# Placing the routing weights of a PEER layer: two fp32r products with the one-hots where one fp32 product stood

## What is computed

```
cand = (v1[..., :, None] + v2[..., None, :]).reshape(TOKEN_CHUNK, PEER_HEADS, PEER_TOPK * PEER_TOPK)
top_s, top_c = lax.top_k(cand, PEER_TOPK)
e1 = jnp.take_along_axis(i1, top_c // PEER_TOPK, axis=-1)
e2 = jnp.take_along_axis(i2, top_c % PEER_TOPK, axis=-1)
expert = e1 * PEER_KEYS + e2
g = jax.nn.softmax(top_s, axis=-1)
u = jnp.take(expert_u, expert, axis=0)
act = jax.nn.gelu(jnp.einsum('thkd,td->thk', u, xc).astype(jnp.float32), approximate=False)
w = (g * act).astype(xc.dtype)
return jnp.einsum('thk,thkd->td', w, jnp.take(expert_v, expert, axis=0))
```

## Time and profile before

| what | us |
|---|---|
| median of 3 runs (lowest, highest) | 2684.39 (2683.01, 2688.0) |
| the profiled execution: its own time | 2680.22 |
| its span, first to last instruction | 2678.4 |
| PE busy in the span | 2513.1 (94%) |
| PE weight loads / DVE / ACT / POOL busy | 2326.6 / 1722.5 / 1218.6 / 1241.4 |
| chain that ended last: share of PE / DVE / POOL | 73% / 8% / 8% |
| placing stretches, layer 0 and layer 1 | 997.4 to 1251.8 and 2053.0 to 2307.3 |

### The profile page before, as it was taken

One profiled execution on the slowest core, in us unless ns is written; L12 is line 12 of the kernel. 1 busy time (PEld: TensorE's weight loads), 2 busy tenths in 40 slices (PEclk: granted clock), 3 DMA queues, 4 the chain that ended last, 5 costly groups with the idle time before them and its releaser, 6 DMA issues.

```text
span 2678.4 us, 45632 instructions
## 1 busy us (share of the span) xinstructions
PE 2513.1 (94%) x17562; PEld 2326.6 (87%) x17562; DVE 1722.5 (64%) x3009; ACT 1218.6 (45%) x2090; POOL 1241.4 (46%) x506
## 2 busy tenths in 40 slices
PE   7998899868789999999999999998999999999998
PEld 6998799858689999999888888888999999988887
DVE  5558487468934976666766774662795666555555
ACT  5334333334434544444444444554544444445444
POOL 4437588625357996665000002446798666300000
PEclk8899899978889999999999998999999999999999
DMA  4325477754245554444877773334555444555664
GB/s 162 95 74 163 133 246 242 259 184 142 63 124 173 181 192 144 149 150 157 268 258 252 251 266 113 104 102 142 179 176 173 150 145 148 167 194 190 192 193 142
DMA packets 125335, 457.84 MB, mean 171 GB/s; under 512 B 13904, under 2 KB 14288, under 8 KB 124752
## 3 DMA queue, kind: packets, MB, share of 16 engines
q1 hardware_dynamic: 124848, 450.73, 52.1%
q10 hardware_dynamic: 288, 4.33, 0.4%
HBM read 453.95 MB, written 1.05 MB: 170 GB/s over the span
## 4 chain that ended last, share of the span: by engine, by line
PE 73%; DVE 8%; POOL 8%; issue 6%; DMA 3%; ACT 2%; POOLq 0%; SPq 0%; DVEq 0%; ACTq 0%
PE ms L1190 26%; PE mm L1152 17%; PE mm L751 16%; POOL low L1683 8%; PE ms L1172 4%; PE mm L758 2%; PE mm L769 1%; DVE work L1716 1%; DMA ring<-w_ffn_up 1%; PE mm L781 1%; DVE work L1722 1%; DMA ring<-w_ffn_down 1%; ACT high L1363 1%; DVE work L2013 1%; DVE parts L1716 1%
## 5 line engine op out<-in xcount | busy, mean ns | idle before, releaser
L1683 POOL TENSOR_TENSOR low<-ring,high 128x1024 fp32r<-128x1024 f32 (+1 forms) x502 | 1241.2, 2486 | 1069.8 <-ACT high L1363 891.7
L1565 ACT ACTIVATE high<-ring 128x1024 fp32r<-128x1024 f32 x506 | 535.9, 1059 | 356.8 <-PE ms L1190 321.7
L1152 PE MATMUL mm<-hs,high 128*128 128x256 f32 x4096 | 524.2, 281 | 3.4 <-ACT high L1363 3.4
L1190 PE MATMUL ms<-high,wts 128*128 128x512 f32 x2048 | 511.1, 392 | 0.0
L1152 PEld LDWEIGHTS mm<-hs,high 128*128 128x128 f32 x4096 | 490.2, 188 | 3.8 <-issue 3.8
L2179 DVE TENSOR_TENSOR low<-ring,high 128x1024 fp32r<-128x1024 f32 x256 | 313.4, 1225 | 248.7 <-ACT high L1565 248.4
L1190 PEld LDWEIGHTS ms<-high,wts 128*128 128x128 f32 x2048 | 384.2, 188 | 83.2
L1363 ACT ACTIVATE high<-ring 128x1024 fp32r<-128x1024 f32 (+1 forms) x252 | 259.1, 1032 | 254.2 <-PE mm L751 109.8
L751 PE MATMUL mm<-hs,high 128*128 128x256 f32 x2608 | 344.8, 287 | 16.5 <-ACT high L1363 16.3
L751 PEld LDWEIGHTS mm<-hs,high 128*128 128x128 f32 x2608 | 324.4, 195 | 21.3 <-ACT high L1363 17.9
L1152 PE MATMUL mm<-hs,low 128*128 128x256 f32 x2048 | 278.5, 278 | 10.1 <-POOL low L1683 9.9
(11 more groups left out here) (285 smaller groups left out, 2888.7 us busy)
## 6 DMA issues: line engine op xcount, KB each, us to landing
ring<-w_peer_experts SPq DMA_DIRECT2D x512, 512.0 KB, 4.2
ring<-w_mod SPq DMA_DIRECT2D x48, 512.0 KB, 4.4
ring<-w_late_mods SPq DMA_DIRECT2D x48, 512.0 KB, 4.4
ring<-w_ffn_up SPq DMA_DIRECT2D x44, 512.0 KB, 4.4
ring<-w_peer_q SPq DMA_DIRECT2D x32, 512.0 KB, 3.4
ring<-w_fox_in SPq DMA_DIRECT2D x32, 512.0 KB, 3.4
ring<-w_lru_in SPq DMA_DIRECT2D x22, 512.0 KB, 4.1
ring<-w_gates SPq DMA_DIRECT2D x16, 512.0 KB, 3.4
```

What stands on the lines that cost most here:

```text
L1152: ins_ = pe.matmul(mm[:, s_ % BANKS, 0:T], w_[:, k * P:(k + 1) * P], hs[:, b_, k, :], start=pass_ == 0 and k == 0, stop=pass_ == 2 and k = ...
L1190: ins_ = pe.matmul(ms[:, 2 * c + half, :], wts[:, s_ % 3, b_, c * P:(c + 1) * P], v_[:, half * 512:(half + 1) * 512], start=s_ == 0 and pa ...
L1565: act.activation(high[:, (q0 + i) % CUT, :], ring[:, n_ % RAW, :], ACT.Copy) \
L1683: pool.tensor_tensor(low[0:rows, cut_slot, 0:width], ring[0:rows, raw_slot, 0:width], high[0:rows, cut_slot, 0:width].bitcast(F32), ALU.su ...
```

## The change

The weights themselves are rounded to an fp32r half (`slot_high`, in the spare tile `wts`) and the rest; both go into `route`, which now has four parts, and both are turned. The first one-hot is multiplied by each half, which gives `onehot` and `onehot_low`, now of type fp32r as the second one-hot is. `place` multiplies each of the two by the second one-hot and adds up in PSUM. What is placed is high + low.

```diff
@@ -58,7 +58,7 @@
 PH = 8
 TOPK = 16
 KEYS = 128
-ROUTE_SMALL = 22 * PH * 16 + 2 * PH
+ROUTE_SMALL = 24 * PH * 16 + 2 * PH
 LEVELS = 7
 MODS = 4
 LATE_MODS = 2 * 24
@@ -445,6 +445,8 @@
         high = sb("high", [P, CUT, SLOT], F32R)
         low = sb("low", [P, CUT, SLOT], F32R)
         x = sb("x", [P, KD, T])
+        with nc.sbuf_tensor("onehots", [P, KD * T], F32R) as onehots_:
+            pass
         scratch = sb("scratch", [P, KD * T])
         con = sb("con", [P, CON_KEPT])
         vec = sb("vec", [P, VECW])
@@ -469,7 +471,7 @@
 
         mm = ctx.enter_context(nc.psum_tensor("mm", [P, BANKS, 512], F32))
         ms = ctx.enter_context(nc.psum_tensor("ms", [P, 4, 512], F32))
-        routeT = ms[:, 0:TT, 0:3 * P].rearrange("p c (s t) -> p c s t", s=3)
+        routeT = ms[:, 0:TT, 0:4 * P].rearrange("p c (s t) -> p c s t", s=4)
 
         def cst(name):
             a_, b_ = CONST0[name]
@@ -595,11 +597,14 @@
         expo = area(TT * PH * 16).rearrange("p (c j k) -> p c j k", c=TT, j=PH)
         sums = area(PH)
         rsums = area(PH)
-        route = area(TT * 3 * P).rearrange("p (c s k) -> p c s k", c=TT, s=3)
+        route = area(TT * 4 * P).rearrange("p (c s k) -> p c s k", c=TT, s=4)
         assert free[0] == KEYS * T and eq_at >= (BEFORE + 2) * T
         placed = work[:, :].rearrange("p (e t) -> p e t", e=KEYS)
         hf = scratch[:, :].rearrange("p (j t) -> p j t", j=KD)
-        onehot = scratch[:, :].rearrange("p (b s i n) -> p b s i n", b=2, s=2, i=4)
+        onehot = onehots_[:, :].rearrange("p (b s i n) -> p b s i n", b=2, s=2, i=4)
+        spare_wts = wts[:, :, :, :].rearrange("p a b t -> p (a b t)")
+        onehot_low = spare_wts[:, 0:8 * P].rearrange("p (b i n) -> p b i n", b=2, i=4)
+        slot_high = spare_wts[:, 8 * P:10 * P].rearrange("p (c k) -> p c k", c=TT)
         value_sums = scratch[:, :].rearrange("p (c d) -> p c d", c=TT)
 
 
@@ -1158,7 +1163,7 @@
 
                     for c in range(TT):
                         pe.wait_ge(sem("routed"), TT * L + c + 1)
-                        for s in range(3):
+                        for s in range(4):
                             ins_ = pe.transpose(routeT[:, c, s, :], route[:, c, s, :], ident)
                         ins_.then_inc(sem("route_turned"), 1)
 
@@ -1169,8 +1174,11 @@
                         pe.wait_ge(sem("place_copied"), GROUPS * L + i - 1)
                         pe.wait_ge(sem("place_weighed"), GROUPS * L + i - 1)
                     for t in range(PLACED):
-                        ins_ = pe.matmul(ms[:, 2 + i % 2, t * P:(t + 1) * P], onehot[:, i % 2, 0, t, :],
-                                         onehot[:, i % 2, 1, t, :], start=True, stop=True, skip_group_check=True)
+                        at = ms[:, 2 + i % 2, t * P:(t + 1) * P]
+                        pe.matmul(at, onehot[:, i % 2, 0, t, :], onehot[:, i % 2, 1, t, :], start=True, stop=False,
+                                  skip_group_check=True)
+                        ins_ = pe.matmul(at, onehot_low[:, i % 2, t, :], onehot[:, i % 2, 1, t, :], start=False,
+                                         stop=True, skip_group_check=True)
                     ins_.then_inc(sem("place_ready"), 1)
 
                 def values(s_):
@@ -2142,7 +2150,9 @@
                         .then_inc(sem("first_onehots"), 1)
                     dve.tensor_tensor(onehot[:, k % 2, 1], numbers, column(1), ALU.is_equal)
                     dve.wait_ge(sem("first_onehots"), GROUPS * L + k + 1)
-                    dve.tensor_tensor(onehot[:, k % 2, 0], onehot[:, k % 2, 0], column(2), ALU.mult) \
+                    first = onehot[:, k % 2, 0].bitcast(F32)
+                    dve.tensor_tensor(onehot_low[:, k % 2], first, column(3), ALU.mult)
+                    dve.tensor_tensor(onehot[:, k % 2, 0], first, column(2), ALU.mult) \
                         .then_inc(sem("onehots"), 1)
 
                 def weigh_placed(k):
@@ -2299,8 +2309,13 @@
                 S.settle()
                 S.did(dve.reciprocal(rsums, sums))
                 S.settle()
-                tt(route[:, c, 2, :].rearrange("p (j k) -> p j k", j=PH), expo[:, c],
-                   rsums.unsqueeze(2).to_broadcast([P, PH, 16]), ALU.mult, "routed")
+                tt(expo[:, c], expo[:, c], rsums.unsqueeze(2).to_broadcast([P, PH, 16]), ALU.mult)
+                S.settle()
+                weights = expo[:, c].rearrange("p j k -> p (j k)")
+                S.did(dve.tensor_copy(slot_high[:, c, :], weights))
+                S.settle()
+                S.did(dve.tensor_copy(route[:, c, 2, :], slot_high[:, c, :].bitcast(F32)))
+                tt(route[:, c, 3, :], weights, slot_high[:, c, :].bitcast(F32), ALU.subtract, "routed")
 
             experts(0)
 
```

## The result

| what | before | changed |
|---|---|---|
| median of 20 runs, us (lowest, highest) | 2681.20 (2674.79, 2688.90) | 2687.48 (2676.21, 2696.43) |
| profiled execution: time, span | 2680.22, 2678.4 | 2693.09, 2691.2 |
| PE / DVE / POOL busy in the span | 2513.1 / 1722.5 / 1241.4 | 2518.8 / 1823.9 / 1241.4 |
| first one-hot product to the last one's start, layers 0 and 1 | 251.5, 251.5 | 251.4, 252.1 |

The ratio is 1.0024, interval 1.0013 to 1.0035: 6.3 us slower. The forecast was 2685, 0.4 us above the kernel before, with 2678 to 2802 as range. The time lies in the range. Its middle is on the slower side of the 0.2% bound (5.4 us), where I had put 0.28, and the interval reaches to both sides of it.

What follows compares the result with a forecast made beforehand. PE, busy throughout the placing stretches, was taken as the bound. Product 0, pace 0, turn +0.4 and DVE 0 took the profiled 2680.22 to 2680.6; from the median, 2684.4 + 0.4, rounded 2685 us, range 2678 to 2802.

Steps and rivals of the forecast that it cites:

- The one-hot product costs its load: PE's placing stretches: each product is paced by loading 128 weight columns, 0.112 to 0.113 us, eight loads staying eight; term 0.
- Rivals on the product: Two rivals on PE's placing: narrow fp32r products slow, +103 to +119 us, chance 0.20; or load hidden, -58 us, chance 0.04.
- narrow fp32r product was slow: PE's eight one-hot products a group: no full fp32r rate at 128 columns, +103 to +119 us, some 2796; chance 0.20.
- The load did not hide: Rival on PE's placing: the fp32r weight load hides, 0.057 us a product, -58 us, about 2627; chance 0.04.
- The 81 ns a pair: PE's one-hot products: skill page's sustained figure for 128 columns; a group would be 0.65 us and the time about 2652.
- The pace of hidden steps, 0: PE's hidden steps behind the groups: fast and slow pace keep alternating as before; 0, bounds -5.8 to +12.7 us.
- always fast: Rival on PE's hidden steps in the placing stretches: never the slow pace, -5.8 us, 2679; chance 0.15.
- always slow: Rival on PE's hidden steps in the placing stretches: slow pace throughout, +12.7 us, 2698; chance 0.08.
- DVE's cover in the stretch: Placing stretches: DVE's fourth one-hot instruction, 0.60 us a group, stays hidden behind PE; DVE busy 203 of 254 us; 0.
- The turn, +0.4: Turn ahead of placing: four more transposes over two layers at 0.11 us each, +0.4 us; DVE's added weight work hidden.
- Copy and subtraction together: DVE's slot_weights before the turn: both pass after one wait for a POOL instruction, so weights just fit in layer 0; 0.
- the turn waits: Rival, layer 0's turn: copy and subtraction wait separately, two more POOL instructions, PE stands 4.5 us, 2689; chance 0.03.

Runs made afterwards that it cites:

- the first experiment: The changed kernel run once more with no edit, beside the kernel before: 2683.77 us, ratio 1.0011 (0.9997 to 1.0025).
- the bf16 kernel: Changed kernel with weights turned whole and cut in halves behind the turn, one-hots and both halves in bf16: 2632.16 us, ratio 0.9800 to the kernel before.
- the third experiment: Kernel before with the changed kernel's rounding, copy and subtraction ahead of the turn and its eight transposes, placing unchanged: 2684.05 us, ratio 1.0013.
- the fifth: The changed kernel with the turn three hidden steps earlier: 2692.33 us, ratio 1.0023 (1.0014 to 1.0032) to the kernel before.
- the last experiment: The changed kernel with the turn one hidden step later: 2686.15 us, ratio 1.0014 (0.9999 to 1.0028) to the kernel before.

## Why the prediction was right in range and short in size

That 2685 came within 2.5 us of 2687.48 is partly luck. It stood on a median of 2684.39 from three runs, and over twenty the kernel before has 2681.20; the change itself was forecast at +0.4 us and measured at +6.3, and at +3.0 in the first experiment.

*The one-hot product costs its load*: right, and the largest question of the case. The term was 0 with bounds of -58 and +119 us; the stretches came out at 251.4 and 252.1 us against 251.5. Leaving a product out gives back 0.112 us and halving its columns nothing. The rule that I had cited, that the number of weight columns sets a load's time (the Trainium skill, "TensorE: Matmul & The Clock Gate", section "LDWEIGHTS (loading the stationary operand)"), holds between fp32 and fp32r, but not for bf16: 98 ns against 192 for the same 128 columns. Another section of that page of the Trainium skill, "Weight-path perf modes — Fast Weight Load (FWL) and DoubleRow", does say that weights can be read 32 bits at a time, two of bf16 and with no win for fp32; the trace agrees with that for bf16, and here fp32r gains nothing either.

*Rivals on the product*: both are refuted. No narrow fp32r product was slow, with 128 or with 64 columns, and I had given that 0.20, most of my 0.28 for slower: the sign came out on that side for another reason. The load did not hide. The 81 ns a pair that I had weighed from the Trainium skill (same page, section "Back-to-back issue gap") is seen for neither type: 112 in fp32r, 55 in bf16.

*The pace of hidden steps, 0*: right between the groups, where the step is slow after one and less so after the next, as before; neither "always fast" nor "always slow" came. But the term looked at the placing only. Behind a turn of eight transposes PE can stay in the slower pace until the first group, as in layer 1 of the first comparison and in both layers of the first experiment, which costs 1.3 to 1.4 us a layer.

*DVE's cover in the stretch*: right, 200.78 us for the expected 203, and PE is not idle there.

*The turn, +0.4*: this is the step that failed. It had three parts. The four transposes are 0.4 us, as said. "Copy and subtraction together" was false: each is held by POOL for itself, which makes the chain two POOL instructions longer, one for each tile, as the rival "the turn waits" had it. And "in layer 1 DVE idles 16.06 us before the turn, 5 more, and so has room" was false in a way that the rival shared: it took the idle time of one execution for a property of the kernel. The chain became 14.2 us longer, which from 16.06 would just fit; the wait came in layer 1 nevertheless, and layer 0, where 10.63 would not have done, had 4.1 us to spare. DVE's idle time before the turn was 18.79 in both layers with the cut behind the turn, and 10.63 and 16.07 in the bf16 kernel, which runs the same instructions ahead of it. And in the changed kernel itself, layer 1's weights came 3.8 us late in the first comparison and 4.1 us early in the first experiment. The lead of DVE over PE varies by 8 us from one execution to another.

I had priced such a wait at 4.5 us for a chance of 0.03. Measured it is 4.0 us, and 2.3 more for the clock in the step behind, which the rival left out; with the slower pace and the transposes, 8.4 us in the two layers of the profiled execution. The medians differ by 6.3, but how many of the executions behind them waited is not known. That the loss is made ahead of the turn and in it, and not by the new products, is borne out by three pairs: with the halves made behind the turn nothing is lost (0.9998); made ahead of it without the new products, they cost (1.0013); with the early turn, they cost 15.6 us (1.0057), most of it in waits that the trace shows, while the kernel before does not mind the early turn (0.9997).

*What stays open.* In the profiled executions of the first and the third experiment PE did not wait, yet their medians are 3.0 and 3.3 us above the kernel before. The traces show 3.2 and 1.8 us of it without any wait, as transposes and slower pace; other executions may have waited besides (each was profiled once). So how the median loss divides between waits and the pace is not shown. Nor is what holds PE in the slower pace. It stayed in it behind the turn in 7 of 16 profiled layers with eight transposes and in none of 8 with six; in two of the seven it was there already ahead of the turn. But eight transposes and DVE's longer chain always came together, and eight transposes with the weights surely in time, or six with late ones, were not tried. The later turn could have told, but its interval holds both.

## What to carry to other kernels

A product with 128 weight columns and few moving ones is paid by its load: count loads, and ask for the type's load time, before splitting or narrowing products; halves in bf16 pay where fp32r halves don't. A few DVE instructions of 0.3 us are not cheap where POOL streams: each of the forms named in the next section waits for one of POOL's, unless an operand is in PSUM. And a reserve read from one profile is one draw; where work is put ahead of a point at which PE may have to wait, hold it against the shortest lead of several executions, and add what the clock takes if PE does wait.

## What the runs showed of the hardware

- A rounding from fp32 to fp32r or a copy in fp32, 128 x 128 from SBUF to SBUF, was held by POOL's instructions as an operation with two SBUF inputs was: 2.28 to 2.33 us, and a subtraction right behind a held copy was held once more (2.44 to 2.50; it took 0.28 where it met a gap between two of POOL's, in layer 0 of the first experiment). With one operand in PSUM, at twice the width, they take 0.42 and 0.43.
- After a wait of 3.8 us in layer 1, PE's granted clock was 0.50 (1.2 GHz) from 2053.90 to 2057.40, and the next hidden step took 5.15 us instead of 2.82; after the waits of 1.2 us in the fifth and the last experiment it took 2.82.
- PE's slower pace, 2.82 us for a hidden step instead of 2.72, also comes at a granted clock of 1.00 and can last from a turn to the first group.
- Loads of 128 columns: 192 ns in fp32 and fp32r, 98 in bf16; products 0.112 and 0.055 us apart. With 64 columns passing instead of 128, fp32r products stay 0.11 us apart.
- The idle time of DVE before the turn, where PE did not wait, fell close to a few values in nearly all layers (4.7, 7.8, 10.6, 13.7, 16.1, 18.8): about one hidden step of 2.72 us apart, so the lead seems to slip by whole steps. Why was not tried.
